# Moving one gathered-row use per pair of groups from quarter 20 to quarter 30 of 32, and two steps of the first norm by a quarter or two, in a hybrid attention, RWKV-7 and PEER block

## What is computed

```python
def chunk(args):
    xc, ic, gc = args                      # tokens, 128 chosen experts of each, their gates
    u = jnp.take(expert_u, ic, axis=0)
    act = jax.nn.gelu(jnp.einsum('cd,cjd->cj', xc, u), approximate=False) * gc
    return jnp.einsum('cj,cjd->cd', act, jnp.take(expert_v, ic, axis=0))
...
x = _layer_norm(DEEPNORM_ALPHA * x + ffn + ple, ln2_w[i], ln2_b[i])
```

## Time and profile before

| what | value |
|---|---|
| timed runs, median (lowest to highest) | 4423.14 us (4422.46 to 4424.35) |
| the profiled execution's own time | 4417.61 us |
| its span | 4415.9 us (1.7 us of the time lie around it) |
| mean granted TensorE clock over the span | 0.978 |
| PE, PEld, DVE, ACT, POOL busy | 94%, 84%, 73%, 35%, 16% of the span |
| the part of the expert stage in which rows are used | about 2423 to 4339 us |

### The profile page before, as it was taken

One profiled execution on the slowest core, in us unless ns is written; L12 is line 12 of the kernel. 1 busy time (PEld: TensorE's weight loads), 2 busy tenths in 40 slices (PEclk: granted clock), 3 DMA queues, 4 the chain that ended last, 5 costly groups with the idle time before them and its releaser, 6 DMA issues. The chain is left out here.

```text
span 4415.9 us, 62390 instructions
## 1 busy us (share of the span) xinstructions
PE 4129.6 (94%) x23580; PEld 3692.5 (84%) x23580; DVE 3211.0 (73%) x4910; ACT 1552.9 (35%) x2731; POOL 701.9 (16%) x580
## 2 busy tenths in 40 slices
PE   8999989988988999898978999999999999999997
PEld 6888875657776877787768999999999999999997
DVE  4444437767836345698195889998989899999987
ACT  2111113436623312222373333333333333333332
POOL 0000001113310100234400111111111111111210
PEclk9999999999999999999999999999999999999998
DMA  9999996886686387664358999999999999999995
GB/s 277 314 313 316 313 268 177 246 250 185 210 233 203 125 261 226 212 204 152 138 154 284 313 327 319 317 317 319 327 311 316 317 324 319 320 319 318 322 314 182
DMA packets 609515, 1176.94 MB, mean 267 GB/s; under 512 B 113992, under 2 KB 363696, under 8 KB 554976
## 3 DMA queue, kind: packets, MB, share of 16 engines
q1 hardware_dynamic: 535424, 800.28, 61.3%
q0 software_dynamic: 54256, 363.92, 21.6%
q10 hardware_dynamic: 19568, 9.18, 0.8%
HBM read 1006.90 MB, written 228.15 MB: 280 GB/s over the span
## 5 line engine op out<-in xcount | busy, mean ns | idle before, releaser
L102 PE MATMUL h_ps<-h_a,h_v 128*128 128x352 f32 x6144 | 1079.3, 324 | 43.3 <-DVE h_a L96 29.0
L102 PE MATMUL h_ps<-xs,h_ut 128*128 128x352 f32 x6144 | 1073.9, 324 | 17.8 <-DVE h_ut L96 17.8
L102 PEld LDWEIGHTS h_ps<-h_a,h_v 128*128 128x128 f32 x6144 | 1002.1, 189 | 55.4 <-DVE h_a L96 36.2
L102 PEld LDWEIGHTS h_ps<-xs,h_ut 128*128 128x128 f32 x6144 | 1006.5, 189 | 19.3 <-DVE h_ut L96 18.6
L102 PE MATMUL a_ps<-xt_hi,a_w 128*128 128x512 f32 x1792 | 553.1, 390 | 8.0 <-DVE a_w L96 8.0
L96 DVE TENSOR_TENSOR h_v<-h_v_raw,h_v 128x512 fp32r<-128x512 f32 x512 | 350.9, 686 | 80.2 <-ACT h_v L95 80.1
L102 PEld LDWEIGHTS a_ps<-xt_hi,a_w 128*128 128x128 f32 x1792 | 337.2, 188 | 78.4 <-issue 8.2
L95 ACT ACTIVATE h_v<-h_v_raw 128x512 fp32r<-128x512 f32 x512 | 318.1, 622 | 187.3 <-PE h_ps L102 181.2
L102 PE MATMUL a_ps<-xt_lo,a_w 128*128 128x512 f32 x896 | 349.3, 390 | 0.0
L2838 DVE SCALAR_TENSOR_TENSOR y_first<-rows,h_acts,y_first 128x2048 f32<-128x2048 f32 x128 | 300.3, 2346 | 0.0
L2832 DVE CUSTOM_DVE_ANT_0 rows<-rows,x_first 128x2048 f32<-128x2048 f32 x128 | 292.5, 2285 | 0.0
(11 more groups left out here) (394 smaller groups left out, 6437.8 us busy)
## 6 DMA issues: line engine op xcount, KB each, us to landing
h_v_raw<-in_peer_v SPq DMA_DIRECT2D x128, 1024.0 KB, 9.8
h_u_raw<-turned_d SPq DMA_DIRECT2D x138, 512.0 KB, 10.2
raw_d<-in_peer_u SPq DMA_DIRECT2D x472, 128.0 KB, 3.7
h_u_raw<-raw_d SPq DMA_DIRECT2D x118, 512.0 KB, 9.7
a_raw<-in_w_in SPq DMA_DIRECT2D x28, 2048.0 KB, 12.7
a_xin<-in_peer_u SPq DMA_DIRECT2D x224, 256.0 KB, 7.9
turned_d<-a_xin SPq DMA_DIRECT2D x56, 1024.0 KB, 6.8
yt_last<-sums_d SPq DMA_DIRECT2D x124, 176.0 KB, 5.2
```

What stands on the lines that cost most here:

```text
L102: mm = pe.matmul(out, lhs[a], rhs[b], start=(first and n == 0), stop=(last and n == 2))
```

## The change

Five edits, all in `experts`:

1. `free`: the eleventh use of every second group stands in quarter 30 of 32 (quarter 14 of its group, the third of a step) in place of quarter 20 (quarter 4 of the group, the first of a step). As quarters are counted from 22, the first such use is at n = 30 and not at n = 52; the last is at n = 478 and not at n = 500. The last use of all stays at n = 507.
2. `GAIN_FIRST` is n = 526 and not 525; the square root on ScalarE stands at the start of quarter 526 and not of 524.
3. `spread_first` on VectorE stands in quarter 525 and not in 523.
4. The large instruction of `gain_first` stands in quarter 526 and not in 525.
5. The reciprocal goes from `gain_first` to `shift_first`, in quarter 527.

No instruction is added or removed.

```diff
-        free = [n for n in range(LATE_USES, Q * STEPS) if n % 16 in SLOTS or n % 32 == 20]
-        ADD_FIRST, GAIN_FIRST, SHIFT_FIRST = Q * STEPS + 8, Q * STEPS + 13, Q * STEPS + 15
+        free = [n for n in range(LATE_USES, Q * STEPS) if n % 16 in SLOTS or n % 32 == 30]
+        ADD_FIRST, GAIN_FIRST, SHIFT_FIRST = Q * STEPS + 8, Q * STEPS + 14, Q * STEPS + 15
         use_at = {n: r for r, n in enumerate(free[:2 * JOBS])}
...
-                    if n == GAIN_FIRST - 1:
+                    if n == GAIN_FIRST:
                         root_first()
...
                 dve.scalar_tensor_tensor(rows[0][:, :], rows[0][:, :], less[:, 0:1], x1[0][:, :], ALU.add, ALU.mult)\
                    .then_inc(gained, 1)
+
+            def shift_first():
                 dve.wait_ge(rooted, 1)
                 dve.reciprocal(var[:, 0:1], var[:, 0:1]).then_inc(inverted, 1)
-
-            def shift_first():
                 dve.wait_ge(inverted, 1)
                 dve.wait_ge(gained, 1)
...
-                    if n == GAIN_FIRST - 2:
+                    if n == GAIN_FIRST - 1:
                         spread_first()
                     if n == GAIN_FIRST:
                         gain_first()
```

## The result

| | before | after |
|---|---|---|
| median of five timed runs | 4423.14 us (4419.73 to 4424.65) | 4445.27 us (4441.17 to 4449.21) |
| ratio | | 1.0047, 95% interval 1.0036 to 1.0058 |
| the profiled execution's own time | 4417.61 us | 4444.76 us |
| first U product of the expert stage starts at | 2338.8 us | 2346.6 us |
| U product of n = 17 to U product of n = 511 (starts, from the timeline) | 1959.3 us | 1980.1 us |

What follows compares the result with a forecast made beforehand. TensorE was taken to bound the expert stage, full except where VectorE is late. Stalls 8.1, clock 15.3 and norm 0 sum to +23.4 us; 4423.14 + 23.4 - 2.8 = 4443.7 us, range 4429 to 4456.

Steps and rivals of the forecast that it cites:

- What bounds the kernel: Expert stage: TensorE is full but for bank waits at quarter 10 and gated-hidden-layer waits at group boundaries, 44.6 us in all.
- Use taken from quarter 20: Quarter 10 of eleven-use groups: VectorE reaches quarter 8's add 2.26 us earlier, all fourteen bank stalls go, -11.5 us.
- Use put into quarter 30: Boundaries after eleven uses: the extra use delays the gating by its full length; all stalls 52.7 us against 44.6, +8.1.
- The `choice` wait on top: Every second boundary, U use in quarter 14: VectorE waits 1.12 us for ScalarE right ahead of the gating.
- The clock: TensorE's clock falls to 1.2 GHz behind long boundary stalls, 1.53 us per fall, +15.3 us in all.
- I take 11: Falls of TensorE's clock expected behind the fourteen long boundary stalls, within bounds of 2 and 14.
- The rival in which the clock holds: Long boundary stalls without lower clock: stalls alone, +8.1, 4431 us; chance 0.13.
- The norm's edits: End of the expert block: the later norm chain is covered by ScalarE's copies, cost 0, bounds -0.5 and +0.4 us.
- The half taken off for the gap between profile and median: Timed runs lie 5.5 us above the profiled execution, perhaps partly from clock falls already paid; 2.8 us taken off.
- Faster, if there is room in quarters 14 and 15: Half of the moved use disappears into slack ahead of the gating: stalls -8.9, clock -1.5, 4412.7 us; chance 0.08.
- Longer stalls by a late row: Moved row late, or clock low for longer: another 1.5 us at each of fourteen boundaries, 4465 us; chance 0.06.

Runs made afterwards that it cites:

- the filled kernel: The changed kernel with the first nine matmuls of the V product made twice at each of the fifteen boundaries, in otherwise idle time: 4429.77 us, ratio 1.0010.
- choice is late: The kernel before with `choice`, ScalarE's gelu and gate after a U use, moved behind u_half and v_half of its quarter: 4383.62 us, ratio 0.9907.

## Why the prediction was right

- **What bounds the kernel.** Right: these two kinds of wait are all that PE shows in that part of either profile, and their +9.0 us with the clock's 12 answer for the +20.8 us of the stretch. (A slip: of the 23 waits at boundaries fourteen come after eleven uses, not fifteen; n = 32 has ten ahead of it before the change, as the prediction itself says further on.)
- **Use taken from quarter 20.** All fourteen bank stalls gone, as forecast (-11.5 us).
- **Use put into quarter 30.** Idle 2.97 us forecast for boundaries with a U use in quarter 14, 2.71 to 3.10 measured, mean 2.98; 2.87 forecast for those with a V use there, 2.85 to 3.08 measured, mean 2.97. At n = 32 3.48 and 3.58. Stalls in all 52.7 us forecast and 53.6 measured, so +9.0 for +8.1. The `choice` wait on top at every second boundary was forecast too, and it is 6.6 of the 9.0 us. n = 64 cost 1.75 where 2.0 was taken. Walking VectorE's queue from a ten-use boundary was good to 0.1 us on the mean.
- **The clock.** The mechanism was right and the count too high: 11 falls taken, 8 seen, one of them in place of the one before. Seven more falls at 1.7 us (from the filled kernel; 1.53 was taken) are 12, and 20.8 - 9.0 = 11.8 us are left for them in the profile, against 15.3 forecast. That term, "I take 11", is the one that was mis-sized. The price of 1.53 us was right for a fall of 3.4 us; three of the eight lasted 6.8 us and cost 2.5 to 2.7. So too few falls and longer ones partly made up for each other, which was luck. The rival in which the clock holds is refuted by the filled kernel. Falls followed stretches of 2.90 us (n = 160) and 2.94 us (n = 352), and none followed the 3.10 us at n = 320 and 448. By the rule of the Trainium skill ("TensorE: Matmul & The Clock Gate", section "Why this matters for your kernels"), no idle gap above about 3 us, the first two should have kept the clock and the last two should not; the measurements decide against it as a line to plan by.
- **The norm's edits.** Cost 0 taken, with bounds -0.5 and +0.4; 0 in the profile after, 0.3 in the kernel that has them alone, where the clock gave less cover, and 0.7 in the filled kernel, beyond the upper bound.
- **The half taken off for the gap between profile and median.** That 4443.7 us lies 1.6 us from the median tests the sum less well than it seems: the medians differ by 22.1 us, and without the 2.8 us the forecast would be 4446.5. The stretch is the test, 20.8 us for a sum of 23.4. The reason given for the 2.8 us did not hold for the most part. The two profiled executions are 27.2 us apart, and 7.8 of these lie ahead of the expert stage, which the change does not touch. The granted clock from 0 to 2320 us, before and then after:

```profile
0.00:2320.00 2320.00, 2119.33 (x11110) 1697.33 (x11111) 1372.64 (x2441) 785.22 (x1102) 358.82 (x251) 0.97 0.76 227
```

```profile
0.00:2320.00 2320.00, 2120.68 (x11068) 1699.63 (x11068) 1365.69 (x2415) 778.42 (x1086) 357.55 (x251) 0.96 0.76 227
```

The profiled execution of before came through those stages quickly (clock 0.97, after 0.96, and a start of the expert stage at the early end of the twelve profiles, 2338.7 to 2348.7 us). That the clock is the cause of the 7.8 us is likely and was not tried. More falls at the 2.1 us stretches do occur (three within the stretch with the norm's edits alone, which has the same uses), so part of the guess stands.
- **The other rivals.** *Faster, if there is room in quarters 14 and 15*: refuted, the rows stand back to back up to the gating at the boundaries shown. *Longer stalls by a late row*: refuted, VectorE shows no idle ahead of any use of a row from 2440 us on. The clock did stay low for longer than 3.4 us, three times.
- **What the working did not see** though it did no harm: the waits in the first quarters of a group, which I had waved off as falling among others, leave about 1.2 us of lateness that goes when choice is late, and together with the one ahead of the boundary they are worth more than the whole change: 1959.3 to 1923.0 us on the stretch of the kernel before.

## What to carry to other kernels

Before moving work to a quarter that looks light, walk the late engine's queue up to the next point where the bottleneck waits for it: if the rows stand back to back, the lateness is handed on in full, and two short stalls become one long one. That by itself cost little here (1.1 us at seven boundaries together). What cost was ScalarE's wait, which the moved use now brought right ahead of the point that TensorE waits for (6.6 us at six), and the lower clock behind the longer idle stretches, about 12 us, more than all that was added to the stalls (9). And look for waits that the late engine gets from its helper's order: putting ScalarE's small, not urgent instruction behind the urgent ones was worth 0.9%, twice the size of the change that was made.

## What the runs showed of the hardware

In the two profiles with the use in quarter 30, nothing filled and choice where it was, the clock fell behind 8 of 14 idle stretches of 2.65 to 3.8 us each; not the same ones (n = 352 and 480 in one, 320 and 448 in the other). It stayed low for 3.4 or for 6.8 us. Behind the filled kernel's thirteen stretches of 1.2 to 2.0 us from n = 96 on it fell not once, while one of seven at 2.0 to 2.1 us was followed by a fall in the kernel before, and three of eight in the one with the norm's steps alone. The shortest idle stretch with a fall behind it is 1.76 us, at n = 224 of the kernel with quarter 13 moved to 0 and choice where it was:

```profile
3205.38 0.75 PE L102 MATMUL h_ps<-h_a,h_v 128*128 128x352 f32 x3 [1.76 <-DVE h_a L96]
...
3206.70:3210.00 3.30, 3.30 (x13) 3.30 (x12) 3.11 (x3) 0.78 (x2) 0.00 (x0) 0.50 0.99 388
```

All idle stretches of over 1 us between about 2430 us and the U product of n = 511, in the twelve profiles together:

| PE idle | stretches | followed by a fall |
|---|---|---|
| 1.0 to 1.7 us | 27 | 0 |
| 1.76 to 2.12 us | 27 | 10 |
| 2.6 to 2.75 us | 4 | 1 |
| 2.85 to 3.13 us | 21 | 12 |
| 3.58 to 3.82 us | 4 | 4 |

All 27 falls there come behind one of these stretches. So in this kernel the length of an idle stretch gives a chance of a fall and not a line between falling and holding. I had expected nearly every stretch of 2.9 us to be followed by a fall.
